# A single-core transformer kernel on Trainium2: all products with the identity that TensorE makes while it waits are taken out

## The reference

```python
# first block
h = rms_norm(x, mix_pre_g[0]); y = conformer_conv_module(h, ...)   # conv of 31 taps, layer norm, silu, @ w_out
x = x + rms_norm(y, mix_post_g[0])
h = rms_norm(x, ffn_pre_g[0]); y = conv_ffn(h, ...)                # 1024 -> 2 * 2816 -> 1024
x = x + rms_norm(y, ffn_post_g[0])
kv = rms_norm(x, kv_norm_g) @ w_kv
# layer 1: dilated attention over kv, then the same kind of conv_ffn
...
# second block
y = token_mixer(...)                                                # mLSTM branch and differential attention
x = x + g1 * y
x = x + g2 * moe_ffn(modulate(rmsnorm(x, norm2_g), sh2, sc2), ...)  # 32 experts, top 4, all weights read
return rmsnorm(x, final_norm_g)
```

## Time and profile before

| | us |
|---|---|
| median of 3 runs | 2382.86 |
| lowest, highest | 2381.7, 2383.41 |
| profiled execution | 2385.08 |
| its span, first to last instruction | 2383.3 |
| mean granted TensorE clock | 0.995 of full speed |
| TensorE busy (matmul) | 2316.8 |

### The profile page before, as it was taken

How to read it: one execution, slowest core, us unless ns; L and a number is a source line. 1 busy time by engine, 2 the same in 40 slices (tenths; PEclk the granted TensorE clock), 3 DMA queues, 4 the chain that set the end, 5 groups by cost and what they waited for, 6 DMA issues and landing times.

```text
span 2383.3 us, 31423 instructions
## 1 busy us (share of the span) xinstructions
PE 2316.8 (97%) x12958; PEld 1747.2 (73%) x12958; DVE 770.5 (32%) x1885; ACT 418.4 (18%) x1026; POOL 0.2 (0%) x4
## 2 busy tenths in 40 slices
PE   8999999999999999999999999999999999999998
PEld 7888888888888888888887787555555555555544
DVE  7734374210434421100355823222222222222212
ACT  5332202010242211100024402111111111111111
POOL 0000000000000000000000000000000000000000
PEclk9999999999999999899999999999999999999999
DMA  6134476654324443234332377999999999999996
GB/s 268 43 133 159 144 296 232 228 222 185 107 89 143 158 148 135 71 115 142 78 125 89 129 285 280 404 427 427 429 428 428 428 428 428 428 428 428 428 427 288
DMA packets 59599, 611.27 MB, mean 256 GB/s; under 512 B 6856, under 2 KB 8264, under 8 KB 10224
## 3 DMA queue, kind: packets, MB, share of 16 engines
q1 hardware_dynamic: 59504, 609.93, 64.4%
HBM read 606.74 MB, written 1.06 MB: 255 GB/s over the span
## 4 chain that ended last, share of the span: by engine, by line
PE 77%; DMA 15%; DVE 7%; issue 1%; ACT 1%; SPq 0%; DVEq 0%; ACTq 0%
PE bank L628 28%; PE bank L1178 14%; PE bank L625 8%; DMA arena<-in_experts 7%; DMA ring<-in_experts 7%; PE bank L716 5%; PE bank L1204 4%; PE bank L642 3%; DVE arena L1809 3%; PE bank L617 2%; PE bank L1169 2%; PE bank L1137 1%; PE bank L727 1%; PE bank L1125 1%; PE bank L747 1%
## 5 line engine op out<-in xcount | busy, mean ns | idle before, releaser
L628 PE MATMUL bank<-arena,ring 128*128 128x256 f32 x3264 | 711.0, 380 | 0.0
L628 PEld LDWEIGHTS bank<-arena,ring 128*128 128x128 f32 x3264 | 622.7, 191 | 83.7
L2240 DVE TENSOR_SCALAR arena<-bank 128x256 f32<-128x256 f32 x64 | 27.2, 425 | 675.4 <-PE bank L1178 675.4
L1178 PE MATMUL bank<-arena 128*64 128x256 f32 x2048 | 231.3, 381 | 14.2 <-DMA arena<-in_experts 14.2
L1178 PE MATMUL bank<-ring,arena 128*64 128x256 f32 x2048 | 233.4, 383 | 5.8 <-DMA ring<-in_experts 5.8
L1178 PEld LDWEIGHTS bank<-ring,arena 128*64 128x64 f32 x2048 | 143.0, 137 | 111.1 <-issue 28.7
L1178 PEld LDWEIGHTS bank<-arena 128*64 128x64 f32 x2048 | 144.4, 137 | 102.9 <-DMA arena<-in_experts 22.5
L625 PE MATMUL bank<-ring,arena 128*128 128x256 f32 x896 | 194.0, 380 | 1.0 <-issue 1.0
L625 PEld LDWEIGHTS bank<-ring,arena 128*128 128x128 f32 x896 | 170.4, 190 | 24.1 <-issue 1.4
L716 PE MATMUL bank<-arena,ring 128*128 128x256 f32 x576 | 124.6, 379 | 0.0
L716 PEld LDWEIGHTS bank<-arena,ring 128*128 128x128 f32 x576 | 109.6, 190 | 14.7
(11 more groups left out here) (301 smaller groups left out, 1905.3 us busy)
## 6 DMA issues: line engine op xcount, KB each, us to landing
arena<-in_experts SPq DMA_DIRECT2D x96, 2048.0 KB, 32.4
ring<-in_experts SPq DMA_DIRECT2D x95, 2048.0 KB, 30.9
ring<-in_dense SPq DMA_DIRECT2D x186, 1024.0 KB, 4.8
ring<-arena SPq DMA_DIRECT2D x16, 128.0 KB, 5.8
con<-in_con SPq DMA_DIRECT2D x1, 1248.0 KB, 12.0
X<-in_x SPq DMA_DIRECT2D x1, 1024.0 KB, 4.9
arena<-in_cond SPq DMA_DIRECT2D x1, 1024.0 KB, 17.5
arena<-in_ctx SPq DMA_DIRECT2D x1, 1024.0 KB, 4.8
```

The costliest lines, as they stand in the source:

```text
L628: ins = nc.tensor.matmul(o, w[:, k, j * P:(j + 1) * P], src[:, k, :], start=(k == 0), stop=(k == KT - 1))
L1178: ins = nc.tensor.matmul(o, XGT[:, k, e * CAP:(e + 1) * CAP], w[:, k, :], start=False, stop=(k == KT - 1), skip_group_check=True)
```

## The change

All 29 calls with the identity are taken out, with the helper and its arguments. No other instruction and no wait is added, moved or removed on any engine; the wait that stood ahead of such a product now stands ahead of the next real one.

```diff
-            def keep_busy(u, count):
-
-                for _ in range(count):
-                    nc.tensor.matmul(half_of(u, 1), ident, C("ident", T), start=True, stop=True)
-
-            def product(u, g, src, token_major=False, wait_chunk=None, busy=0):
+            def product(u, g, src, token_major=False, wait_chunk=None):
...
                 if wait_chunk:
-                    keep_busy(u, busy)
                     for k in range(KT):
                         wait_chunk(k)
...
                 unit_half(pe, u - UNIT_BANKS, 2)
-                keep_busy(u, 2)
                 pe.wait_ge(sem(name + "_diag"), before(name + "_diag") + 1)
...
-            stage("cm_out", H, "ln_h", busy=6)
+            stage("cm_out", H, "ln_h")
             part_spread("n1", FIRST_UNIT["ffn0_in"])
-            stage("ffn0_in", H, "n2_h", count=1, busy=3)
+            stage("ffn0_in", H, "n2_h", count=1)
...
-            stage("kv", H, "n4_h", count=1, busy=5)
+            stage("kv", H, "n4_h", count=1)
...
-            stage("ffn1_in", H, "n7_h", count=1, busy=3)
+            stage("ffn1_in", H, "n7_h", count=1)
...
             units_read(pe, "wo")
-            keep_busy(FIRST_UNIT["wo"] + 2, 4)
 
             pe.wait_ge(sem("chosen"), 1)
...
-            keep_busy(FIRST_UNIT["wo"] + 3, 2)
...
-            for _ in range(2):
-                nc.tensor.matmul(banks[2][:, 0:T], ident, C("ident", T), start=True, stop=True)
             pe.wait_ge(sem("n11_diag"), before("n11_diag") + 1)
```

More of the change, by code:

```diff
@@ L630, in product, with stage @@
                 ins.then_inc(sem(f"unit{u % UNIT_BANKS}"), 1)
-            def stage(name, src, ready=None, token_major=False, first=0, count=None, busy=0):
+            def stage(name, src, ready=None, token_major=False, first=0, count=None):
                 n = SLABS_OF[name] if count is None else count
@@ L635, in stage @@
                     wait = (lambda k: pe.wait_ge(sem(ready), before(ready) + k + 1)) if ready and i == first else None
-                    product(FIRST_UNIT[name] + i, SLAB_AT[name, i], src, token_major, wait, busy)
+                    product(FIRST_UNIT[name] + i, SLAB_AT[name, i], src, token_major, wait)
             def half_product(o, g, j):
```

## The result

The changed kernel takes 2391.64 us (median of 9 runs, 2387.37 to 2392.64), the kernel before 2382.86 us (9 runs, 2381.59 to 2384.97). The ratio is 1.0035, with a 95% interval of 1.0026 to 1.0043: slower by about 8.3 us (6.2 to 10.2). It was forecast slower, with 2387.8 us, a range from 2382.0 to 2392.0, and chances of 0.51 for slower against 0.47 for no change. The sign held, though the forecast had hardly committed to it; the measured time lies inside the range, near its upper end. The loss came out at 1.7 times the forecast 4.9 us.

What follows compares the result with a forecast made beforehand. TensorE bounds the kernel until the expert-weight DMA stream, which starts when TensorE gets there. Terms 1.4 + 2.0 - 0.5 + 2.0 = +4.9 us took 2385.08 to 2390.0, or 2387.8 us at the median; range 2382.0 to 2392.0.

Steps and rivals of the forecast that it cites:

- What the products cost before: At every place but kv, the identity products cost nothing and their removal saves nothing; only at kv do they delay anything.
- the very end: Last product, L1254: ready when VectorE is, perhaps at low clock, but as before; 0 us.
- That the clock falls at cm_out, n1, n6 and in the router: Without the calls the clock halves there: 3 chances in 4 at cm_out, nearly certain at the others.
- cm_out: TensorE idles 3.4 us, then a likely clock fall slows the 128 records behind: +1.4 us (0 to 2.7).
- n1 and n6: Only one-column products and waits for 4.4 us, so the clock falls: +1.0 us at each, +2.0 together.
- kv: Real products begin earlier, though the clock falls with or without the change: -0.5 us (-1.4 to +0.3).
- router: Nothing dense for 3.6 us, so the clock falls ahead of the gather and first experts: +2.0 us (0.5 to 2.7).
- a late return: After a fall the clock comes back late, as behind the gates: 2.7 us lost at a place, not 1.65.
- rival 2: The clock comes back late everywhere: +10.0 us in all, 2392.9 us, about 2391.5 with one place spared; chance 0.18.
- The step from the profiled execution to the median: The 2390.0 us forecast for the profiled execution was lowered by its 2.2 us above the median, to 2387.8 us.
- Rival 3: Only long waits without any product lower the clock, so only cm_out and kv count: +1.2 us, 2384.1; chance 0.17.
- Rival 4: The products never held the clock up and only delay kv: up to 1.4 us gained, 2381.5; chance 0.10.

Runs made afterwards that it cites:

- f0: Kernel before with 27 of its 29 identity calls (all but the two at the end) making one column, not 256: 2390.53 us, ratio 1.0031.
- f3: Kernel before with only the six router calls making one column in place of 256: 2385.00 us, ratio 1.0009.
- g1: Kernel before without the six calls at cm_out, but with six one-column calls made slightly earlier, so later code keeps its place: 2385.01 us, ratio 1.0006.
- f1: Kernel before with only the six calls ahead of cm_out making one column in place of 256: 2385.10 us, ratio 1.0010.
- f2: Kernel before with only the ten calls at n1, ffn0_in, n6 and ffn1_in making one column in place of 256: 2386.69 us, ratio 1.0014.
- e3: Kernel before with only the five calls ahead of kv taken out: 2383.82 us, ratio 1.0002.
- g3: Kernel before with the gates' 32 products of 16 columns made in pairs between the sixteen slab products ahead of them: 2378.35 us, ratio 0.9980.
- e1: Kernel before with only the six calls ahead of cm_out taken out: 2420.34 us, ratio 1.0160.
- e2: Kernel before with only the ten calls at n1, ffn0_in, n6 and ffn1_in taken out: 2411.65 us, ratio 1.0118.
- e4: Kernel before with only the six router calls taken out: 2419.17 us, ratio 1.0150.
- g4: Kernel before with the kv calls moved ahead of the slab wait and the gate products paired between slab products: 2378.88 us, ratio 0.9979.

## Why the prediction came out as it did

**What the products cost before.** Right for the profiled execution. Nowhere but at kv did the real products begin earlier without them; each of the other waits is now as long as the calls and the old idle together. At the very end the calls can cost up to about 1 us where the clock is low, as said above.

**That the clock falls at cm_out, n1, n6 and in the router.** Right, and shown apart from the instructions by f0 to f3. It isn't certain at each place in each execution: g1 has no fall at cm_out, where the forecast had given it 3 chances in 4.

**Sizes.** Here the working was too low. By the ratios of f1, f2, f3 and e3, against the terms of the sum:

| place | term | measured |
|---|---|---|
| cm_out | +1.4 | +2.4 (0.2 to 4.5) |
| n1 and n6 | +2.0 | +3.3 (1.2 to 5.5) |
| kv | -0.5 | +0.5 (-1.7 to 2.6) |
| router | +2.0 | +2.1 (0.0 to 4.3) |
| sum | +4.9 | +8.3 (6.2 to 10.2), the change itself |

The intervals of the single places hold their terms, that of the sum does not. The single places can be read more sharply within the traces. The time from a fixed product ahead of a place to a fixed one behind it agrees within 0.2 us in all traces in which the place is as before (but for kv in g3, where the clock did not fall), so what is above it is the place's price in that execution:

| place, from and to | wide calls in place | low stretch of 3.4 us | low stretch of 6.8 us |
|---|---|---|---|
| cm_out, L668 to the first L686 | 34.9 | +1.6, +1.8, +1.8 (f1, e1, after) | +2.9 (f0) |
| n1, the first L686 to L676 | 13.2 | +0.5, +0.8 (e2, after) | +1.3, +1.5 (f0, f2) |
| kv, the first L701 to L676 | 14.9 to 15.1, low for 3.4 us | | +0.2, +0.6, +0.7 (e3, after, f0) |
| n6, the first L686 to L676 | 13.1 | +0.4 (f2) | +1.5, +1.6, +1.7 (f0, after, e2) |
| router, the second L1085 to L1178 | 9.5 | +1.5, +1.5, +1.5 (e4, f0, after) | +2.0 (f3) |

With g1, which had no low stretch at cm_out and lost 0.1 us, these are 20 cases in which a place went without wide calls. The step that was mis-sized is the length of a low stretch. The forecast took one of 3.3 us, a loss of 1.65, as the rule and a late return as the exception; 10 of the 20 cases have one of 6.8 us and 9 one of 3.4. When it begins goes with how long it lasts: the ten long ones began 0.8 to 3.7 us before the first of the wide products behind the wait (f2 at n1: at 140.3, L617 at 142.17), the nine short ones at most 0.5 us before them or behind their start (the changed kernel at cm_out: at 110.4, L611 at 109.75). What decides when it begins, no run shows.

At kv the term was wrong in sign for that reason. The products start earlier, but 6.8 us at half clock cost more than that gives back: L676 comes 0.2 to 0.7 us later in all three traces without wide calls, where 0.8 earlier was the likeliest case. That is rival 2, which had 0.18, in a milder form: it gave +10.0 in all, the runs +8.3.

**The step from the profiled execution to the median.** The sum was made against a profiled execution, 2.2 us above the median, and those 2.2 us were then taken off as for any execution. The profiled pair differs by 5.6 us and the medians by 8.8. Of these 3.2 us, 1.7 are the luck at the gates. The fall at kv, by contrast, was not luck: of nine traces with the calls at kv as before (before, e1, e2, e4, f1, f2, f3, g1, g3) eight have the low stretch of 3.4 us there. The rest of the 3.2 us stays open, since only one execution of each kernel is traced.

**Rivals 3 and 4.** Rival 3 (only long waits count) falls by f2 and f3. The Trainium skill (TensorE: Matmul & The Clock Gate, Why this matters for your kernels) advises against long idle gaps between bursts. The traces bear that out at cm_out (an idle of 3.54 us, a fall in two executions of three) and at kv (3.97 us, a fall). As the only case it is too narrow here: short waits in a row (1.20 and 1.67 us at n1), and products of one column without a pause (the router of f3), do the same. Rival 4 (the products never held the clock up) falls by f0 alone.

**What was not foreseen.** That a part of the change could cost four times the whole, by the place of the loop. The changed kernel, with 27 calls fewer ahead of the loop, was spared this by luck; nothing in the forecast had looked at it.

## What to carry to other kernels

Before a short chain of dependent steps on other engines, look at what TensorE multiplies in it, not at whether it is busy: if the traces show the clock down behind such a place, wide products can fill it at no cost as long as they end before the next real one is ready (at kv they didn't). Better still, the thin products that the kernel needs anyway can be mixed in among wide ones, as in g3. When a change of a few instructions ahead of a long loop moves the time by far more than its work, compare the instruction packets of the two pages before looking for a reason in the change. And to test one part of such a change, keep the instruction count and change the size of the work.

## What the runs showed of the hardware

The expert loop's instructions stay at hand or are fetched anew in every turn, by a shift of its code of a few calls: with 0, 5 and 27 calls taken out ahead of it there are 68, 68 and 67 instruction packets, with 6 and 10 there are 122, and TensorE loses 7.8 to 8.4 us per turn at the jump (e1, e4) or 5.4 us on average in two pieces (e2). Six turns cost 47.6 us of stalls on TensorE in e1 and about 35 us in the time; the 20 us that TensorE otherwise waits for expert weights in the loop (g1's view of waits) are gone in e1. The clock then falls there too, for 6.8 or 10.2 us in each turn of e1. Which places of the code are good was not mapped, nor how many instructions are kept. That the fetching is what TensorE waits for was not shown by itself; the stalls and the packets came and went together in all fourteen traces.

An idle of 3.54 us left the clock at full in one execution (g1) and brought it to half in two others (e1 and the changed kernel). The clock also fell while TensorE was busy throughout: at the gates, with products of 16 columns, in all twelve traces that make them in one block (6.8 to 13.7 us at half), and in f3's router behind 3.40 us without a pause. Mixed in among products of 256 columns, the same products of 16 columns left it at full in both traces (g3, g4).
